# A hybrid transformer block: order of the first transfers, of one bank's release, and of three small steps at the head of its first attention

## The chip, the cores and the metric

The kernel runs on one core of one Trainium2 chip. The metric is the device time of one execution in microseconds; three executions of the kernel before took 2060.63 us in the median (2058.62 to 2062.41). All times below are in us from the first instruction of one profiled execution unless they are marked as ns.

Five engines work from queues of their own: TensorE (PE, matrix products), VectorE (DVE), ScalarE (ACT), GpSimd (POOL, here mostly an issuer of transfers) and SyncE (SP, here the issuer of all weight transfers). They meet only through semaphores.

## The reference, cut to what matters

One sequence of 256 tokens with 1024 features goes through two layers of a first model (latent attention and dilated attention, each with a modulated norm and an MLP), and then through a second block with a recurrent mixer, cross attention and a large expert layer. The change touches only the beginning of the first layer:

```python
cond = silu(c)
mod = (cond @ ada_w[0] + ada_b[0]).reshape(B, 6, D)      # shift1, scale1, gate1, ...
h = rms_norm(x, norm_mix[0]) * (1 + scale1) + shift1
proj = h @ w_in                                          # 1024 -> 384 + 256 + 32
q_lat, kv_lat, k_rope = split(proj);  k_rope = rope(k_rope, pos)
q  = (rms_norm(q_lat, g_qa) @ w_qb)                      # 16 heads of 96
kv = (rms_norm(kv_lat, g_kva) @ w_kvb)                   # 16 heads of 64 + 64
```

Attention over 16 heads, its output projection, and everything else follow.

## The kernel before, in words

All of it is one straight program for each engine, written out by hand; no scheduler moves anything. Activations are kept transposed: `xT` holds the input as 8 pieces of 128 features by 256 tokens. Every weight matrix is cut into units of up to 128x1024. SP loads unit u into one of four raw buffers (`weights(u)`, which from the fifth unit on waits until the split of unit u-3 is done), ACT copies it into a rounded high part `wh` (L1338), and DVE takes the rest into a low part `wl` (L1957). PE forms each product as high times high, high times low and low times high. The split runs two units ahead of the products.

**The start.** ACT issues five small transfers (L1431 to L1435): the condition as a column `c_col` (4 KB), the constants `con` (265 KB, among them a 128x128 block of ones and the identity), the positions `posI` (1 KB), the vectors `vec` (106.5 KB, biases and gains) and the condition as rows `cond` (512 KB). SP issues the input `xT`, and then the modulation weights and the first weight units (`early` and `weights`, L2876 and L2881).

**The first norm.** ACT squares features 0 to 511 of `xT` and DVE features 512 to 1023, both into `na` (marks `("n0","sq",0)` and `("n0","sq",1)`). PE sums the squares over the features with eight products by the block of ones; a float32 product stands in the trace as two matmuls, so these are 16. ACT and DVE make the root from it, and DVE scales `xT` into `na`.

**The modulation.** For feature pieces 0, 1, 3 and 5 the shift and the scale are made on PE (`ada(j)`, 8 products with `c_col`, 16 matmuls in the trace, then `columns(j)`). For pieces 2, 4, 6 and 7 DVE makes them by two multiply-and-sum instructions of 128x1024 on the weights in `first` (`products(j)`, L1940). PE runs sum of squares, `ada(0)`, `ada(1)`, `columns(0)`, `columns(1)`, `ada(3)`, `w_in(0)`, `columns(3)`, `w_in(1)`, `ada(5)`, `w_in(2)`, and so on to `w_in(7)`. Each `w_in(k)` needs the normed piece k in a high and a low part (`high(k)` on ACT, `low(k)` on DVE).

**The latent stage.** The eight `w_in` steps add up five latent tiles in five PSUM banks (`lat` 3 and 4 for keys and values, 0 to 2 for queries; bank 2 holds the raw rotary key as well). ACT and DVE take each tile out as a high and a low part (`latTh`, `latTl`), ACT squares the tiles, PE sums the squares (`lat_sums`), and the roots follow (`lat_root`). PE then runs the four units of `w_kvb`, two groups of products each (`kvb`, s, t), with the sums of squares and the turning of the rotary key (`k_rope`, L818) in between. ACT takes each group out with the root as its scale (mark `("kvb","v",s,t)`).

**The banks.** PSUM has eight banks. `take` in the tensor program takes the bank that stands first in a line of free banks and waits for whoever must have read it; `give` puts a bank at the end of the line, with the mark to be waited for. Which bank, and thus which wait, a step gets depends on the order of all `give` calls before it. Around the change the line is used so: `("kvb",0,0)` takes bank 3, the sums for keys and values bank 4, `("kvb",0,1)` bank 5, `k_rope` bank 6 (which held `lat` 3), `("kvb",1,0)` bank 7 (which held `lat` 4), and the sums for the queries bank 3.

**POOL** starts its own transfers only when the last of the sixteen `early` transfers has landed.

Of the kernel before, what the change touches and what calls it, by code (L numbers as in the profile page):

```python
# [8 lines left out]
ALU = mybir.AluOpType  # L9
# [537 lines left out]
def tensor_program(e, b, S, at):  # L547
    pe = Engine(e)
# [4 lines left out]
    def take(*name):  # L553

        i, sem, key = free.popleft()
        if sem is not None:
            pe.wait_ge(sem, at[key])
        at[("bank",) + name] = i
        return b.psum[:, i, :]

    def give(*name, sem, key):
        free.append((at[("bank",) + name], sem, key))

    def mm(o, l, r, start, stop, mark=None, loose=False):
        i = e.matmul(o, l, r, start=start, stop=stop, skip_group_check=loose)  # L565
        if mark:
            i.then_inc(S.pe, 1)
            n[0] += 1
            at[mark] = n[0]
# [195 lines left out]
    def mla():  # L765
        m = b.mla
# [68 lines left out]
        def kv(s):  # L835
            j = weights("mla_w_kvb", s)
            for t in range(2):
                ps = take("kvb", s, t)
                for k in range(2):
                    pe.wait_ge(S.dve, at["lat", "lo", 3 + k])  # L840
                    l, r = sp(m.latT, 3 + k, 256, t * 128, 128), wsp(j, k * 512, 512)
                    mm(ps, l[0], r[0], k == 0, False)
                    mm(ps, l[0], r[1], False, False)
                    if t == 1 and k == 1:
                        e.matmul(ps, l[1], r[0], start=False, stop=True).then_inc(S.unit, 1)
                    else:
                        mm(ps, l[1], r[0], False, k == 1, mark=("kvb", s, t) if k == 1 else None)
                if (s, t) == (0, 0):
                    for c in (3, 4):
                        give("lat", c, sem=S.act, key=("lat", "square", c))  # L850
                give("kvb", s, t, sem=S.act, key=("kvb", "v", s, t))
                if (s, t) == (0, 0):
                    lat_sums("kv", (3, 4), 0)
                if (s, t) == (0, 1):
                    k_rope()
                if (s, t) == (1, 0):
                    lat_sums("q", (0, 1, 2), 1)
# [83 lines left out]
            give("mla", "oT", c, sem=S.dve, key=("mla", "out", c))  # L941

        pe.wait_ge(S.c_con, 16)
        ps = take("n0", "sum")
        for k in (0, 1, 2, 3, 4, 5, 6, 7):
            if k < 4:
# [372 lines left out]
def scalar_program(e, b, S, at, d):  # L1319
# [5 lines left out]
    def act(o, i, f, mark=None, **kw):  # L1325
        e.activation(o, i, f, **kw).then_inc(S.act, 1)  # L1326
        n[0] += 1
        if mark:
            at[mark] = n[0]
        return n[0]  # L1330
# [98 lines left out]
    def mla():  # L1429
        m = b.mla  # L1430
        e.dma_start(m.ccol, d["c_col"]).then_inc(S.c_col, 16)  # L1431
        e.dma_start(b.con, d["con"]).then_inc(S.c_con, 16)
        e.dma_start(m.posI, d["pos_col"]).then_inc(S.pos_col, 16)
        e.dma_start(b.vec, d["vec"]).then_inc(S.c_vec, 16)
        e.dma_start(b.cond, d["c_row"]).then_inc(S.c_cond, 16)  # L1435
        ac.wait_ge(S.c_col, 16)
        act(m.ccol, m.ccol, ACT.Silu, mark="c col")
        ac.wait_ge(S.c_x, 16)
        act(m.na[:, 0:1024], b.xT[:, 0:1024], ACT.Square, mark=("n0", "sq", 0))
        ac.wait_ge(S.c_cond, 16)  # L1440
        act(b.cond, b.cond, ACT.Silu, mark=("cond",))
        ac.wait_ge(S.dve, at["angles"])
        act(m.trig, m.trig, ACT.Sin, mark=("trig",))
        ac.wait_ge(S.c_con, 16)
        norm_tail("n0", 8, m.ntmp)
        ac.wait_ge(S.c_vec, 16)

        def row(j):
            ac.wait_ge(S.pe, at["ada done", j])
# [39 lines left out]
        ac.wait_ge(S.unit, u + 1)  # L1489
        lat_high(2)  # L1490
        act(m.krT[0:32, :], bank("lat", 2)[0:32, 256:512], ACT.Copy, mark="k rope in")
        lat_root("kv", 2, 256)
        for c in range(3):
            lat_square(c)

        def head_root(key, z):
            h = m.hs[key]
# [414 lines left out]
def vector_program(e, b, S, at):  # L1912
# [15 lines left out]
    def tt(o, x, y, f, mark=None):  # L1928
        return op(e.tensor_tensor(o, x, y, f), mark)  # L1929
# [203 lines left out]

    def mla():
        m = b.mla
        ve.wait_ge(S.c_x, 16)
        tt(m.na[:, 1024:2048], b.xT[:, 1024:2048], b.xT[:, 1024:2048], ALU.mult, mark=("n0", "sq", 1))
        ve.wait_ge(S.c_con, 16)
        ve.wait_ge(S.pos_col, 16)
        cp(m.pos, m.posI)  # L2140
# [19 lines left out]
        ts(m.trig, m.trig, 3.1415925, -3.1415925, ALU.min, ALU.max, mark="angles")  # L2160
        ve.wait_ge(S.c_vec, 16)
        stt(m.more, vc(b, "ada_b", 8, 8), 1.0, vc(b, "norm_mix", 0, 8), ALU.add, ALU.mult)

        def product(c, slot):
            u = m.first[:, slot * UNIT:(slot + 1) * UNIT]
# [34 lines left out]
        for j in range(8):  # L2200
            if j >= 3:
                ada(j)
            ahead(j - AHEAD)
            low(j)
            if j in (1, 2, 3):
                products({1: 4, 2: 6, 3: 7}[j])
        unit("mla_w_in", 6)
        unit("mla_w_in", 7)

        def lat_low(c):  # L2210
            ve.wait_ge(S.act, at["k rope in"] if c == 2 else at["lat", "hi", c])
# [17 lines left out]
        for c in (3, 4, 0, 1, 2):  # L2229
            lat_low(c)  # L2230
        lat_root("kv", 2)
        ve.wait_ge(S.act, at["trig",])
        sin, cos = m.trig[:, 0], m.trig[:, 1]
        for h in range(2):
            cp(m.cs[:, :, 16 * h:16 * h + 16], cos)
        ts(m.sn[:, :, 0:16], sin, -1.0, None, ALU.mult)
        cp(m.sn[:, :, 16:32], sin)

        def kv(s):
            unit("mla_w_kvb", s)  # L2240
# [628 lines left out]
def sync_program(e, b, S, at, d, out):  # L2869
# [16 lines left out]
        early(2 * j + 1)  # L2886
    for j in range(3):
        weights(j)
    early(6)
    early(7)  # L2890
    weights(3)
    for i in range(8, 16):
        early(i)
    for j in range(4, 8):
        weights(j)
    for u in range(8, len(PLAN)):
        weights(u)
# [231 lines left out]
```

## Time and profile before

| | |
|---|---|
| median of three executions | 2060.63 us (2058.62 to 2062.41) |
| the profiled execution | 2060.63 us, of which its span is 2058.8 us |
| PE busy | 1983.9 us, 96% of the span |
| DVE busy | 1409.6 us, 68% |
| ACT busy | 1140.9 us, 55% |
| POOL busy | 302.1 us, 15% |
| mean granted PE clock | 0.984 of full |

The span runs from the first to the last instruction; 1.8 us of the execution lie around it. A PE that is shown busy is not PE at its peak, since matmuls are pipelined and their ends are modelled; what can be read well is when a matmul starts and whether PE waited before it. The stretch that the change touches is the first 60 us of the 2059.

### The profile page before, as it was taken

What the parts mean: (1) busy time and instruction counts of PE and PEld (TensorE: products, weight loads), DVE (VectorE), ACT (ScalarE), POOL (GpSimd) and SP (SyncE); (2) the same over time, 40 slices, a digit from 0 to 9 for tenths busy, and PEclk for the clock granted to TensorE, in tenths of its full rate; (3) what the DMA queues carried; (4) which work ended last, traced back from release to release, by engine and by line L of the source; (5) the groups of instructions that cost most, each with busy time, mean ns of one, the idle gap of its engine ahead of it and who ended that gap; (6) DMA issues with size and microseconds to landing.
All of it is one profiled execution on the core that took longest, in us unless ns stands there. A gap on an engine that the chain in (4) does not pass through costs nothing.

```text
span 2058.8 us, 34870 instructions
## 1 busy us (share of the span) xinstructions
PE 1983.9 (96%) x14212; PEld 1834.5 (89%) x14212; DVE 1409.6 (68%) x2543; ACT 1140.9 (55%) x1919; POOL 302.1 (15%) x328
## 2 busy tenths in 40 slices
PE   8998998999999989998898989999999999999997
PEld 5898998998888889997788989999999998888886
DVE  6777765888677567547646458999997765555554
ACT  5855533556766455435554444457767754444444
POOL 0010000000000000000000000018876950000000
PEclk9999999999999999999999999999999999999999
DMA  9465787346444347664334345554444445555553
GB/s 352 164 206 183 246 283 236 114 162 213 148 144 157 97 127 226 189 188 166 132 103 143 124 145 165 183 183 147 153 154 154 144 146 189 188 185 191 186 186 120
DMA packets 97743, 356.25 MB, mean 173 GB/s; under 512 B 11104, under 2 KB 11232, under 8 KB 97200
## 3 DMA queue, kind: packets, MB, share of 16 engines
q1 hardware_dynamic: 84240, 305.04, 44.5%
q0 software_dynamic: 12624, 48.08, 7.2%
q8 instruction: 112, 1.84, 0.3%
q10 hardware_dynamic: 720, 0.91, 0.1%
q14 instruction: 47, 0.39, 0.1%
HBM read 352.94 MB, written 1.05 MB: 172 GB/s over the span
## 4 chain that ended last, share of the span: by engine, by line
PE 91%; DVE 4%; ACT 3%; issue 1%; DMA 1%; ACTq 0%; DVEq 0%; POOL 0%
PE psum L572 24%; PE psum L574 24%; PE psum L573 23%; PE psum L565 18%; PE psum L579 2%; DVE wl L1957 1%; ACT work L1326 0%; ACT wh L1338 0%; DMA araw<-in_ada_w 0%; DVE C L1937 0%; DMA con<-in_con 0%; ACT L1326 0%; DVE araw L1940 0%; DVE mlp_sq L1937 0%; DVE cross_sq L1937 0%
## 5 line engine op out<-in xcount | busy, mean ns | idle before, releaser
L1957 DVE TENSOR_TENSOR wl<-raw,wh 128x1024 fp32r<-128x1024 f32 (+1 forms) x566 | 687.5, 1218 | 437.8 <-ACT wh L1338 437.1
L1338 ACT ACTIVATE wh<-raw 128x1024 fp32r<-128x1024 f32 (+1 forms) x566 | 593.6, 1050 | 444.3 <-PE psum L574 407.3
L572 PE MATMUL psum<-peer_hh,wh 128*128 128x256 f32 x1152 | 332.8, 289 | 4.2 <-DVE peer_hl L1929 4.0
L574 PE MATMUL psum<-peer_hh,wl 128*128 128x256 f32 x1152 | 326.2, 283 | 0.0
L573 PE MATMUL psum<-peer_hl,wh 128*128 128x256 f32 x1152 | 324.1, 281 | 0.0
L572 PEld LDWEIGHTS psum<-peer_hh,wh 128*128 128x128 f32 x1152 | 217.4, 189 | 5.4 <-issue 4.4
L573 PEld LDWEIGHTS psum<-peer_hl,wh 128*128 128x128 f32 x1152 | 219.9, 191 | 0.0
L574 PEld LDWEIGHTS psum<-peer_hh,wl 128*128 128x128 f32 x1152 | 216.6, 188 | 0.0
L572 PE MATMUL psum<-wh,csh 128*128 128x512 f32 x512 | 202.9, 396 | 0.0
L574 PE MATMUL psum<-wh,csl 128*128 128x512 f32 x512 | 202.7, 396 | 0.0
L573 PE MATMUL psum<-wl,csh 128*128 128x512 f32 x512 | 202.7, 396 | 0.0
L2848 POOL TENSOR_SCALAR C<-con,selT 128x128 f32<-128x128 f32 x128 | 135.2, 1069 | 194.9 <-DVE selT L1944 172.8
L572 PE MATMUL psum<-mlp_hh,wh 128*128 128x256 f32 x512 | 148.3, 290 | 8.3 <-DVE mlp_hl L1937 8.3
L573 PE MATMUL psum<-mlp_hl,wh 128*128 128x256 f32 x512 | 146.2, 286 | 0.0
L574 PE MATMUL psum<-mlp_hh,wl 128*128 128x256 f32 x512 | 146.2, 286 | 0.0
L573 PE MATMUL psum<-h1l,wh 128*128 128x256 f32 x512 | 144.1, 281 | 0.0
L572 PE MATMUL psum<-h1h,wh 128*128 128x256 f32 x512 | 144.1, 281 | 0.0
L574 PE MATMUL psum<-h1h,wl 128*128 128x256 f32 x512 | 144.1, 281 | 0.0
L2774 POOL DMA_DIRECT2D araw<-in_ada_w x76 | 40.1, 529 | 692.6 <-DVE mod L1940 662.1
L574 PEld LDWEIGHTS psum<-wh,csl 128*128 128x128 f32 x512 | 96.4, 188 | 23.4
L573 PEld LDWEIGHTS psum<-wl,csh 128*128 128x128 f32 x512 | 96.3, 188 | 23.4
L572 PEld LDWEIGHTS psum<-wh,csh 128*128 128x128 f32 x512 | 96.3, 188 | 23.3
(455 smaller groups left out, 4675.3 us busy)
## 6 DMA issues: line engine op xcount, KB each, us to landing
raw<-in_mlp_w SPq DMA_DIRECT2D x128, 512.0 KB, 4.1
raw<-in_eu SPq DMA_DIRECT2D x128, 512.0 KB, 3.5
raw<-in_ev SPq DMA_DIRECT2D x128, 512.0 KB, 3.4
araw<-in_ada_w POOLq DMA_DIRECT2D x76, 512.0 KB, 4.8
raw<-in_dil_qk SPq DMA_DIRECT2D x48, 512.0 KB, 3.6
raw<-in_dil_v SPq DMA_DIRECT2D x24, 512.0 KB, 3.6
raw<-in_w_in SPq DMA_DIRECT2D x16, 512.0 KB, 3.4
raw<-in_w_query SPq DMA_DIRECT2D x16, 512.0 KB, 3.5
```

Of the source, the lines that this page charges most:

```text
L565: i = e.matmul(o, l, r, start=start, stop=stop, skip_group_check=loose)
L572: e.matmul(o, l[0], r[0], start=start, stop=False, skip_group_check=loose)
L573: e.matmul(o, l[0], r[1], start=False, stop=False, skip_group_check=loose)
L574: i = e.matmul(o, l[1], r[0], start=False, stop=stop, skip_group_check=loose)
L579: t = e.transpose(o, i, ident)
L1338: e.activation(b.wh[v % NSPLIT][:, 0:cols], b.raw[v % NRAW][:, 0:cols], ACT.Copy).then_inc(S.hi, 1)
L1957: e.tensor_tensor(b.wl[v % NSPLIT][:, 0:cols], b.raw[v % NRAW][:, 0:cols], b.wh[v % NSPLIT][:, 0:cols].bitcast(F32), ALU.subtract).then_in ...
L2774: e.dma_start(b.araw[i % 2], d["ada_w"][first + c]).then_inc(S.ada[i % 2], 16)
L2848: e.tensor_scalar(o1[:, i, :], iota, m.selT[:, 0, t:t + 1], m.selT[:, 2, t:t + 1], ALU.is_equal, ALU.mult).then_inc(S.pool, 1)
```

## The change

It has five parts. In the first, ACT issues `posI` ahead of `con`, and `cond` ahead of `vec`. In the second, PE waits for `vec` as well as `con` before its sum of squares, ACT waits for `con` and `vec` before it squares its half of `xT`, and DVE squares its half only after the angles of the rotary embedding and one small instruction on `vec`. In the third, SP issues the later `early` transfers in pairs between weight units, where before all of them went ahead of the fifth unit; DVE's `products(6)` and `products(7)` are each one step later. In the fourth, four small DVE copies of sine and cosine move from behind the key root to ahead of the `latTl` steps, and ACT squares the three query tiles before it makes the key root, not behind it. In the fifth, the bank of `("kvb",0,0)` is given back ahead of the banks of `lat` 3 and 4.

```diff
@@ tensor program
+                give("kvb", s, t, sem=S.act, key=("kvb", "v", s, t))
                 if (s, t) == (0, 0):
                     for c in (3, 4):
                         give("lat", c, sem=S.act, key=("lat", "square", c))
-                give("kvb", s, t, sem=S.act, key=("kvb", "v", s, t))
-                if (s, t) == (0, 0):
                     lat_sums("kv", (3, 4), 0)
@@
         pe.wait_ge(S.c_con, 16)
+        pe.wait_ge(S.c_vec, 16)
         ps = take("n0", "sum")
@@ scalar program
         e.dma_start(m.ccol, d["c_col"]).then_inc(S.c_col, 16)
+        e.dma_start(m.posI, d["pos_col"]).then_inc(S.pos_col, 16)
         e.dma_start(b.con, d["con"]).then_inc(S.c_con, 16)
-        e.dma_start(m.posI, d["pos_col"]).then_inc(S.pos_col, 16)
+        e.dma_start(b.cond, d["c_row"]).then_inc(S.c_cond, 16)
         e.dma_start(b.vec, d["vec"]).then_inc(S.c_vec, 16)
-        e.dma_start(b.cond, d["c_row"]).then_inc(S.c_cond, 16)
         ac.wait_ge(S.c_col, 16)
         act(m.ccol, m.ccol, ACT.Silu, mark="c col")
+        ac.wait_ge(S.c_con, 16)
+        ac.wait_ge(S.c_vec, 16)
         ac.wait_ge(S.c_x, 16)
         act(m.na[:, 0:1024], b.xT[:, 0:1024], ACT.Square, mark=("n0", "sq", 0))
...
-        lat_root("kv", 2, 256)
         for c in range(3):
             lat_square(c)
+        lat_root("kv", 2, 256)
@@ vector program
-        ve.wait_ge(S.c_x, 16)
-        tt(m.na[:, 1024:2048], b.xT[:, 1024:2048], b.xT[:, 1024:2048], ALU.mult, mark=("n0", "sq", 1))
         ve.wait_ge(S.c_con, 16)
         ve.wait_ge(S.pos_col, 16)
...
         stt(m.more, vc(b, "ada_b", 8, 8), 1.0, vc(b, "norm_mix", 0, 8), ALU.add, ALU.mult)
+        ve.wait_ge(S.c_x, 16)
+        tt(m.na[:, 1024:2048], b.xT[:, 1024:2048], b.xT[:, 1024:2048], ALU.mult, mark=("n0", "sq", 1))
...
-            if j in (1, 2, 3):
-                products({1: 4, 2: 6, 3: 7}[j])
+            if j in (1, 3, 4):
+                products({1: 4, 3: 6, 4: 7}[j])
@@ sync program
-    early(6)
-    early(7)
-    weights(3)
-    for i in range(8, 16):
-        early(i)
-    for j in range(4, 8):
+    for j in range(3, 8):
+        early(2 * j)
+        early(2 * j + 1)
         weights(j)
```

At the very start of ACT's program its instructions change as follows (`na` is the buffer of the squares; the names in brackets are the semaphores waited for, `s_vec` and `s_con` those of the two transfers).

```order
@@ -1,18 +1,17 @@
-L2938 UNCONDITIONAL_BRANCH [waits barrier_Pool_Activation_PE_DVE_SP_release]
+L2935 UNCONDITIONAL_BRANCH [waits barrier_Pool_Activation_PE_DVE_SP_release]
 L1431 DMA c_col<-in_c_col 128x8
-L1432 DMA con<-in_con 128x530
-L1433 DMA posI<-in_pos_col 128x2
-L1434 DMA vec<-in_vec 128x213
-L1435 DMA cond<-in_c_row 128x1024
+L1432 DMA posI<-in_pos_col 128x2
+L1433 DMA con<-in_con 128x530
+L1434 DMA cond<-in_c_row 128x1024
+L1435 DMA vec<-in_vec 128x213
```

The vectors are now the last of the five transfers, and the constants the third. On PE the first matmul of the program, the sum of squares, reads so:

```order
-L565 MATMUL psum<-na,con 128x256 [waits s_act,s_con]
+L565 MATMUL psum<-na,con 128x256 [waits s_act,s_vec,s_con]
 L565 MATMUL psum<-na,con 128x256 x3
 L565 MATMUL psum<-na,con 128x256 [waits s_dve]
```

Nothing is moved there; one more semaphore is waited for. Further on, DVE's steps between the splits of the last `w_in` units (`wl`) and the first split of the `kvb` stage stand so (`cos_cos` and `minus_plus_sin` are the copies for the rotary embedding, `latTl` the low parts of the latent tiles, `lat_sums` the key root):

```order
@@ -62,10 +62,10 @@
 L1929 TENSOR_TENSOR mla_hl<-na,mla_hh 128x256
 L1957 TENSOR_TENSOR wl<-raw,wh 128x1024 x2
+L1944 COPY cos_cos<-trig 128x2x16 x2
+L1933 TENSOR_SCALAR minus_plus_sin<-trig 128x2x16
+L1944 COPY minus_plus_sin<-trig 128x2x16
 L1937 SCALAR_TENSOR_TENSOR latTl<-psum,vec,latTh 128x256 x5
 L1929 TENSOR_TENSOR lat_sums<-lat_sums 128x2
 L1937 SCALAR_TENSOR_TENSOR lat_sums<-lat_sums 128x2 x2
-L1944 COPY cos_cos<-trig 128x2x16 x2
-L1933 TENSOR_SCALAR minus_plus_sin<-trig 128x2x16
-L1944 COPY minus_plus_sin<-trig 128x2x16
```

Four instructions are moved ahead of the five `latTl` steps. On ACT, in the same place of the program:

```order
 L1326 ACTIVATE latTh<-psum,vec 128x256 x3
 L1326 ACTIVATE ntmp<-psum 32x256
+L1326 ACTIVATE lat_squares<-psum 128x256 x3
 L1326 ACTIVATE lat_sums<-psum,con 128x2
 L1326 ACTIVATE lat_sums<-lat_sums 128x2
-L1326 ACTIVATE lat_squares<-psum 128x256 x3
 L1338 ACTIVATE wh<-raw 128x1024
 L1326 ACTIVATE kv<-psum,lat_sums 128x512 x2
```

The three squares stand ahead of the two steps of the key root. PE's own order in this stage is the same before and after, but the line of free banks isn't: `k_rope` now gets bank 3, which waits for ACT's copy of `("kvb",0,0)` (the first `kv<-psum,lat_sums` above), where before it got bank 6, which waits for the square of `lat` 3. `("kvb",1,0)` gets bank 6, and the query sums bank 7.

## Rows read from the trace of the kernel before

**Rows 1.** Waits of PE in the first 100 us: total, times, longest (us).

```profile
PE psum L565 <- DMA con<-in_con: 8.0, 1, 8.0
PE psum L579 <- ACT na L1326: 1.5, 1, 1.5
PE psum L565 <- DVE latTl L1937: 0.8, 1, 0.8
PE psum L789 <- ACT ada_row L1326: 0.3, 1, 0.3
```

**Rows 2.** Timeline of PE: start, length, instruction, idle before and its releaser.

```profile
8.00 6.27 PE L565 MATMUL psum<-na,con 128*128 128x256 f32 x16 [8.00 <-DMA con<-in_con]
14.19 7.07 PE L565 MATMUL psum<-first,c_col 128*1 128x256 f32 x32
```

**Rows 3.** First PE row in two narrow windows, from 9.0 and from 9.5.

```profile
9.01 1.49 PE L565 MATMUL psum<-na,con 128*128 128x256 f32 x3
9.44 1.49 PE L565 MATMUL psum<-na,con 128*128 128x256 f32 x3
```

**Rows 4.** Busy time by stretch: PE, PEld, DVE, ACT, POOL, PE clock, DMA share, GB/s.

```profile
10.00:20.00 10.00, 10.00 (x40) 5.41 (x39) 6.96 (x21) 3.63 (x6) 0.00 (x0) 1.00 1.03 416
```

**Rows 5.** Timeline of ACT and its queue, and of DVE, in the first 15 us.

```profile
2.13 0.83 ACTq L1434 DMA_DIRECT2D vec<-in_vec  x1
5.97 1.04 ACT L1326 ACTIVATE na<-xT 128x1024 f32<-128x1024 f32 x1
13.83 1.06 ACT L1326 ACTIVATE cond<-cond 128x1024 f32<-128x1024 f32 x1 [6.83 <-DMA cond<-in_c_row]
...
9.74 0.17 DVE L1944 CAST pos<-posI 128x2 f32<-128x2 int32 x1 [2.84 <-DMA posI<-in_pos_col]
```

**Rows 6.** Transfers issued, first 14 us: queue, count, size, us from issue to landing.

```profile
vec<-in_vec ACTq DMA_DIRECT2D x1, 106.5 KB, 9.1
```

**Rows 7.** Timelines of DVE and PE, 20 to 31 us; a transfer that nothing delays.

```profile
22.57 0.85 DVE L1957 TENSOR_TENSOR wl<-raw,wh 128x672 fp32r<-128x672 f32 x1
30.36 3.61 PE L565 MATMUL psum<-first,c_col 128*1 128x256 f32 x16
...
raw<-in_ev SPq DMA_DIRECT2D x128, 512.0 KB, 3.4
```

**Rows 8.** Timelines of DVE and PE, 33 to 41 us.

```profile
33.82 1.22 DVE L1940 CUSTOM_DVE_ANT_0 first<-first,cond 128x1024 f32<-128x1024 f32 x1
36.49 0.42 DVE L1929 TENSOR_TENSOR mla_hl<-na,mla_hh 128x256 fp32r<-128x256 f32 x1 [0.35 <-ACT mla_hh L1326]
40.82 0.27 PE L565 MATMUL psum<-mla_hh,wh 128*128 128x256 f32 x1
```

**Rows 9.** Timeline of DVE, 47 to 52 us.

```profile
47.56 0.87 DVE L1937 SCALAR_TENSOR_TENSOR latTl<-psum,vec,latTh 128x256 fp32r<-128x256 f32 x2
...
49.25 1.44 DVE L1937 SCALAR_TENSOR_TENSOR latTl<-psum,vec,latTh 128x256 fp32r<-128x256 f32 x3 [0.82 <-ACT latTh L1326]
...
51.64 0.26 DVE L1944 COPY cos_cos<-trig 128x32 f32<-128x32 f32 x2
...
51.90 0.17 DVE L1944 COPY minus_plus_sin<-trig 128x32 f32<-128x32 f32 x1
```

**Rows 10.** Timeline of ACT, 50 to 54 us.

```profile
50.64 0.26 ACT L1326 ACTIVATE lat_sums<-psum,con 128x2 f32<-128x2 f32 x1 [0.47 <-PE psum L565]
...
51.05 0.91 ACT L1326 ACTIVATE lat_squares<-psum 128x256 f32<-128x256 f32 x3
51.84 1.07 ACT L1338 ACTIVATE wh<-raw 128x1024 fp32r<-128x1024 f32 x1
52.78 1.28 ACT L1326 ACTIVATE kv<-psum,lat_sums 128x512 f32<-128x512 f32 x2
```

**Rows 11.** Timeline of PE, around 52 us.

```profile
52.02 0.30 PE L818 MATMUL psum<-con,ntmp 32*128 32x32 f32 x2
```

**Rows 12.** Busy time by stretch, as in rows 4, further on.

```profile
350.00:400.00 50.00, 44.31 (x340) 42.95 (x341) 43.04 (x94) 28.41 (x62) 1.59 (x3) 0.93 0.32 105
```

More of the change, by code:

```diff
@@ L1443, in mla @@
         act(m.trig, m.trig, ACT.Sin, mark=("trig",))
-        ac.wait_ge(S.c_con, 16)
         norm_tail("n0", 8, m.ntmp)
-        ac.wait_ge(S.c_vec, 16)
         def row(j):
@@ L2204, in mla @@
             low(j)
-            if j in (1, 2, 3):
-                products({1: 4, 2: 6, 3: 7}[j])
+            if j in (1, 3, 4):
+                products({1: 4, 3: 6, 4: 7}[j])
         unit("mla_w_in", 6)
+        ve.wait_ge(S.act, at["trig",])
+        sin, cos = m.trig[:, 0], m.trig[:, 1]
         unit("mla_w_in", 7)
+        for h in range(2):
+            cp(m.cs[:, :, 16 * h:16 * h + 16], cos)
+        ts(m.sn[:, :, 0:16], sin, -1.0, None, ALU.mult)
+        cp(m.sn[:, :, 16:32], sin)
         def lat_low(c):
@@ L2231, in mla @@
         lat_root("kv", 2)
[L2232 to L2237, printed above, removed]
         def kv(s):
```

## The prediction

> **What bounds the kernel now.** I read four views in this order: PE's waits in the first 100 us, PE's timeline there, the timelines of ACT and DVE beside it, and the transfers. PE's waits [rows 1] are a short list: 8.0 us at the start until the constants have landed, and then only 0.8 us on DVE's `latTl`, 1.5 us on ACT's exponentials and 0.3 us on a row. From 8.00 to 47 us PE goes from one matmul to the next. So each microsecond by which PE's first matmul moves is a microsecond of the end, unless some later wait on a fixed time swallows it; and the waits of that list are all on work that itself starts from PE. Between 10 and 20 us PE is busy 10.00 of 10.00 us, and the transfers run at 416 GB/s with their engines full [rows 4]. The transfers are thus the scarce thing of the first microseconds, but PE doesn't wait for them after 8.00.
>
> **First part: PE starts later.** Before, PE needs the constants and the two halves of squares. ACT's half starts at 5.97 and takes 1.04 [rows 5], so it is done by 7.0, and the constants are last, at 8.00 [rows 2]. After the change three things stand ahead of the first matmul: ACT's queue loads the vectors last; ACT squares only when they are there; PE waits for the squares.
>
> When do the vectors land? Before, ACT's five transfers land in the order of issue: constants 8.0, positions 9.7 (the cast that waits for them starts at 9.74), vectors 2.13 + 9.1 = 11.2, and the condition rows 13.8 [rows 2, 5, 6]. Each is some 2 us behind the one ahead, 1 KB of positions nearly like 265 KB of constants, so what counts is that they stand in one line beside SP's full queue. The five are the same after, and SP issues the same up to that time; only the order within the line differs. The last of the line therefore still lands at about 13.8, and the last is now `vec`: it moves from 11.2 to 13.8. This rests on the rows. The Trainium skill's DMA: Bandwidth & Descriptors (section on the SWDGE path, Arbitration) says the same as a mechanism: an engine round-robins between the queues packet by packet, and takes each queue's descriptors in order. The same page (HWDGE ordering) warns that a later transfer's semaphore may complete ahead of an earlier one's; no row here shows that, and I carry it as the fourth rival.
>
> ACT then squares: 13.83 + 1.04 = 14.87. A semaphore takes some 0.06, so PE starts at 14.93. DVE's half (1.2 us, behind a 0.16 us step on `vec`) ends at 15.2, and PE asks for it only four products later. PE's start moves by 14.93 - 8.00 = **6.93 us**.
>
> Nothing takes this back. The sum (16 matmuls, 6.27 us), `ada(0)` and `ada(1)` (32, 7.07 us) follow back to back [rows 2] and ask for nothing sooner than before; ACT's condition step ends at 15.9 and DVE's `products(2)` at 18.3, ahead of the sum's end at 21.2. The sum itself is uncertain. Its matmuls start 0.43 us apart [rows 3], those of `ada` 7.07/32 = 0.22, though the granted clock is shown as 1.00 of 2.4 GHz in the stretch of rows 4: the first matmuls run at half pace whatever that column says. If all 16 ran at 0.43 the sum would take 6.9 (+0.6), if all ran at 0.22 it would take 3.5 (-2.8). I take 6.27 again, since PE comes out of idleness in both. The skill's TensorE: Matmul & The Clock Gate (Part 1) has it that the throttled state is the default, activity releases it, and the number of slow matmuls varies from run to run; the slow pitch agrees, the granted column doesn't, and the sum stays with the rows.
>
> **Second part: SP's order, and `products` one step later.** The fifth weight unit waits until DVE's first split is done, 22.57 + 0.85 = 23.4 [rows 7], and now six `early` transfers are queued behind that wait, and behind three more like it. With the shift the first gate opens at 30.4. Behind it go 0.34 + 0.52 + 0.52 = 1.39 MB up to the pair for `ada(5)`; at 416 GB/s they take 3.3 us. A transfer of 512 KB that nothing delays lands 3.4 us after its issue [rows 7], 1.3 of which are its bytes at that rate, so some 2 us are latency, and the pair is there at 36.0. `ada(5)` starts at 30.36 + 6.93 = 37.3 [rows 7]. Slack 1.3 us. The last pair, three times 1.39 MB behind the gate, is there at 30.4 + 2 + 10.0 = 42.4, against `products(7)` behind `low(4)` at 36.49 + 0.3 + 6.93 = 43.7 [rows 8]. Slack 1.3 us.
>
> On DVE, `products(7)` (two instructions of 1.15 us) now stands between `low(4)` and `ada(5)`. DVE is free for it at 36.6 (unshifted), ends at 38.9, and three short steps (`ada(5)` on DVE, the high part on ACT, the low part on DVE) take some 1.7 us, as an estimate from the lengths of 0.2 to 0.6 us of such steps; the low part is there at about 40.6. `w_in(5)` starts at 40.82 [rows 8]. It fits by 0.2 us; the two steps behind it have more. I take 0. If either slack is gone, the price is what the pair is late: up to 2 us. Below nothing it can't come, since PE has no wait there to lose.
>
> POOL's start hangs on the last pair and comes about 2 us later against PE; its first use lies behind the latent stage. 0.
>
> **Third part: the latent stage.** PE ends `w_in` and waits 0.8 us for DVE's first `latTl`, which starts at 47.56 [rows 1, 9]. DVE now does the four sine and cosine copies first. Their starts are (51.90 - 51.64)/3 = 0.09 apart [rows 9], together 0.35 us, and all of it lies on PE's wait: +0.35. They could have stood in DVE's idle time ahead of its last split, but they are placed behind it.
>
> Then the bank. PE reaches `k_rope` at 52.02 [rows 11], after this change at 52.37. It now takes bank 3 and must wait for ACT's copy of the first `kvb` group. That copy starts at 52.78 and the two take 1.28 [rows 10], so the first ends at 53.4. Is it later than before, as the squares now stand ahead of the root? Before: root 0.41 us from 50.64, squares, and the split at 51.84. After: the squares wait for the last `latTl` (49.25 + 1.44 + 0.35 = 51.05 [rows 9]) and end at 51.45, the root follows until 51.85, the split starts as before. DVE's part of the root takes 0.5 (from ACT's end at 51.1 to the copies at 51.64 [rows 9]) and is done at 52.4, ahead of the split's end. So the copy still starts at 52.78, and its end plus a semaphore is 53.45. `k_rope` moves from 52.02 to 53.45: **+1.43 us** for the stage, 0.35 of it the copies. As a bound, if ACT's root is 0.5 later than I think, +1.9; if the copy is early, +1.1. The steps behind it take banks whose owners are done by then (the query sums take bank 7, whose square is made at the start of the stage), and PE runs on to 84 us without a wait in the list of before, so it is not given back.
>
> **The sum.** 6.93 + 0 + 1.43 = 8.36 us. The profiled execution before took 2060.63 us (span 2058.8 and 1.8 around it), the same as the median, so the forecast is 2069.0 us, 0.4% slower.
>
> **The rivals.**
> 1. The bank costs nothing, because ACT's copy comes sooner or PE is later anyway. For it: ACT has idle gaps ahead of 50.64 [rows 10]. Against it: the copy stands behind a split that is bound to its place. Then 2060.6 + 6.9 + 0.35 = 2067.9.
> 2. SP's gates bind: `ada(5)` or `products(7)` waits for its pair, and PE with it. For it: slacks of 1.3 and 0.2 us, and transfers with full engines. Price 2 us, so 2071.0. It decides where the pair lands later than 37.3.
> 3. Not slower: the PE clock. In nine of the 50 us stretches the mean granted clock is 0.93 to 0.97, as from 350 to 400 [rows 12]. 0.07 of 50 us is 7 us at half the clock, 1.2 GHz, so up to 3.5 us of work lost in each, some 30 us in all. A program that starts 8.4 us later might meet them otherwise; it decides at three of nine. Against it: each fall follows gaps of PE that move with PE, and three executions before lie within 3.8 us. Then 2060 or less. The skill's clock gate section, by which the point of change varies between runs, is the rule behind it.
> 4. `vec` overtakes the condition rows, whose piece of the line is 13.8 - 11.2 = 2.6 us. Then PE starts at 12.3, and the time is 2066.4. Against it: the four rows of the line.
>
> **How the numbers follow.** Forecast 0.73; rival 1 0.09; rival 2 0.09; rival 3 0.03; rival 4 0.06. The forecast's own range is 2066.8 to 2071.0 (sum of squares at -1.5 to +0.6, the stage at +-0.4, the median of three at +-1.5). Taking in rivals 1, 2 and 4 mostly, the range is 2066.0 to 2072.0. What a measurement can tell from no change is 0.2%, 4.1 us. All but rival 3 lie above 2064.7; leaving a part of rival 4 and of the spread: slower 0.93, within 0.2% 0.05, faster 0.02.
>
> **What would show it.** In the profile after: PE's first matmul at 14.9 with ACT's square as releaser (before 12.5: rival 4); ACT idle before its square until a transfer at 13.8; `ada(5)` at 37.3 without a wait (with one: rival 2); the first `latTl` at 54.8, PE's wait before it 1.2; a wait of 1.1 us ahead of `k_rope` at L818 with ACT's `kv` as releaser (none: rival 1). From 60 us on the two traces should differ by a constant 8.4. A constant that shrinks at a stretch with a fallen clock would speak for rival 3. I am wrong if PE starts by 9, or if something behind 100 us waits on a fixed time.

## The result and the profile after

The changed kernel takes 2071.78 us in the median of five executions (2069.62 to 2076.44), the kernel before beside it 2061.64 us. The ratio is 1.0055, 95% interval 1.004 to 1.0072: slower, by 10 to 11 us where 8.4 were forecast. The profiled execution took 2069.42 us (span 2067.6), 8.8 more than the one of before and a little less than the lowest of the five.

PE's waits in the first 110 us of the changed kernel, columns as in [rows 1]:

```profile
PE psum L565 <- ACT na L1326: 15.2, 1, 15.2
PE psum L565 <- DVE latTl L1937: 3.0, 1, 3.0
PE psum L579 <- ACT na L1326: 1.5, 1, 1.5
PE psum L818 <- ACT kv L1326: 1.0, 1, 1.0
PE psum L565 <- DVE mla_hl L1929: 0.6, 1, 0.6
PE psum L789 <- ACT ada_row L1326: 0.3, 1, 0.3
```

Against [rows 1] the start is 15.2 and not 8.0, the wait for `latTl` 3.0 and not 0.8, and two waits are new: 1.0 at `k_rope` (L818) and 0.6 in the `w_in` stage. The start and `k_rope` were forecast. The 0.6 and most of the 3.0 were not.

The start, from the timeline of ACT (as in [rows 5]):

```profile
14.00 1.06 ACT L1326 ACTIVATE na<-xT 128x1024 f32<-128x1024 f32 x1 [8.04 <-DMA vec<-in_vec]
```

from the timeline of PE (as in [rows 2]):

```profile
15.20 5.50 PE L565 MATMUL psum<-na,con 128*128 128x256 f32 x16 [15.20 <-ACT na L1326]
20.62 7.07 PE L565 MATMUL psum<-first,c_col 128*1 128x256 f32 x32
```

and from the list of transfers issued in the first 14 us (as in [rows 6]):

```profile
vec<-in_vec ACTq DMA_DIRECT2D x1, 106.5 KB, 11.0
```

ACT issues the vectors at 2.88, so they land at 2.88 + 11.0 = 13.9, and PE starts at 15.20. The sum of squares takes 5.50 us, not 6.27, so `ada(0)` begins 20.62 - 14.19 = 6.43 later.

Then DVE's timeline, where the rows of before had no wait on a transfer (as in [rows 8]):

```profile
39.39 1.22 DVE L1940 CUSTOM_DVE_ANT_0 first<-first,cond 128x1024 f32<-128x1024 f32 x1 [2.50 <-DMA first<-in_ada_w]
...
46.18 0.84 DVE L1957 TENSOR_TENSOR wl<-raw,wh 128x672 fp32r<-128x672 f32 x1
```

and ACT's, at the split of the second `kvb` unit:

```profile
54.35 1.06 ACT L1338 ACTIVATE wh<-raw 128x1024 fp32r<-128x1024 f32 x1 [2.31 <-DMA raw<-in_mla_w_kvb]
```

DVE waits 2.5 us for `products(6)`' first transfer, so `products(7)` and the split of the sixth `w_in` unit behind it (46.18, before 37.19) are late, and PE waits 0.56 for the low part of that piece. SP issues the second `kvb` unit only when this split is done, at 47.05. ACT gets it at 54.35, 7.3 us after its issue, where 512 KB took 3.4 alone [rows 7]. What stood between is POOL. Its queue's timeline:

```profile
44.27 1.23 POOL L2805 DMA_DIRECT2D ada_piece<-in_ada_k  x2 [43.84 <-DMA first<-in_ada_w]
45.49 1.05 POOL L2774 DMA_DIRECT2D araw<-in_ada_w  x2
```

SP's, at the second `kvb` unit:

```profile
47.05 0.33 SPq L2876 DMA_DIRECT2D raw<-in_mla_w_kvb  x1
```

What each queue moved (packets, MB, share of the 16 engines; q1 is SP's, q0 POOL's), first from 46.9 to 48, then from 49 to 50, then from 51 to 52 us:

```profile
q0 software_dynamic: 87, 0.33, 90.9%
...
q0 software_dynamic: 111, 0.42, 105.8%
...
q1 hardware_dynamic: 53, 0.22, 52.7%
q0 software_dynamic: 60, 0.21, 52.6%
```

POOL's four transfers (2 MB) are issued when the last `early` transfer has landed, at 43.84, and that now comes just ahead of the second `kvb` unit. Up to three microseconds after SP's issue POOL's queue still has the engines for itself.

The kernel before had the same collision, which its rows of waits don't show. POOL's start, SP's issue of the second `kvb` unit, and that unit's time to landing:

```profile
33.81 1.22 POOL L2805 DMA_DIRECT2D ada_piece<-in_ada_k  x2 [33.38 <-DMA first<-in_ada_w]
...
38.07 0.33 SPq L2876 DMA_DIRECT2D raw<-in_mla_w_kvb  x1
...
raw<-in_mla_w_kvb SPq DMA_DIRECT2D x1, 512.0 KB, 6.4
```

There the second unit landed at 44.5 and ACT took it at 45.32; the first, issued at 36.17, took 6.9 us and landed at 43.1, and ACT took it at 43.21. Both came just in time. In the changed kernel the second unit is issued 47.05 - 38.07 = 8.98 us later, 2.55 more than the start's 6.43, and takes 0.9 us longer; that is more than there was to spare.

The last rows are PE's at the first product of the `kvb` stage and at `k_rope` (as in [rows 11]):

```profile
57.55 0.48 PE L565 MATMUL psum<-wh,latTh 128*128 128x512 f32 x1 [2.99 <-DVE latTl L1937]
...
62.44 0.31 PE L818 MATMUL psum<-con,ntmp 32*128 32x32 f32 x2 [0.96 <-ACT kv L1326]
```

**How the shift runs.** All kernels split the same 566 weight units on DVE (`wl`, one instruction each), so the start of split n less the start of the same split in the kernel before tells how late a kernel is at that place. The text calls this the shift. Each column is one profiled execution against the one of before, in us (e6 is told at its own place):

| split (its start before) | after | e1 | e2 | e3 | e4 | e5 | e7 | e8 | e9 | e10 | e11 | e12 |
|---|---|---|---|---|---|---|---|---|---|---|---|---|
| 3rd `w_in` (27.5) | 6.43 | 6.70 | -0.14 | 6.00 | -1.10 | 7.37 | 6.20 | -0.96 | -0.57 | -1.12 | -0.51 | -0.90 |
| 2nd `kvb` (46.4) | 9.02 | 6.70 | 1.70 | 5.99 | 1.10 | 7.98 | 9.38 | -0.27 | 0.43 | 0.70 | 0.30 | 1.02 |
| 1st `qb` (60.2) | 10.41 | 6.73 | 4.78 | 7.37 | 2.96 | 9.37 | 13.95 | -0.23 | -1.65 | -1.38 | 0.30 | -1.06 |
| last (2041) | 8.80 | 5.60 | 6.37 | 8.07 | 0.98 | 7.45 | 16.29 | 0.43 | -0.85 | -1.22 | -1.09 | -2.36 |

The change costs 10.4 us by 60 us, and the profiled execution gives 1.6 back over the other 2000 us, in steps between stretches where it moves with a constant distance. From 60 us to the end nearly every kernel drifts by one or two us either way, whatever was edited, so the row at 60 us is the one to read for the edits and the medians are the ones to read for the time.

### The profile page after: what moved, and what is told of

It reads as the page before. It is cut to its first block, busy times and chain, and to the rows that moved or that the text cites. A ratio compares the mean times of both kernels' runs of the same rounds, so it can differ in the third digit from the quotient of the medians.

```text
span 2067.6 us, 34869 instructions
## 1 busy us (share of the span) xinstructions
PE 1983.9 (96%) x14212; PEld 1833.6 (89%) x14212; DVE 1410.4 (68%) x2543; ACT 1141.0 (55%) x1919; POOL 302.9 (15%) x328
## 4 chain that ended last, share of the span: by engine, by line
PE 88%; DVE 6%; ACT 3%; DMA 2%; issue 1%; ACTq 0%; DVEq 0%; SPq 0%
PE psum L572 23%; PE psum L574 23%; PE psum L573 23%; PE psum L565 16%; PE psum L579 2%; DVE wl L1957 1%; ACT wh L1338 1%; DMA vec<-in_vec 1%; ACT work L1326 0%; DMA first<-in_ada_w 0%; DMA araw<-in_ada_w 0%; DMA raw<-in_mla_w_kvb 0%; ACT na L1326 0%; DVE mix_sq L1937 0%; ACT L1326 0%
```

## The experiments

Medians are over all executions of a kernel, with the ratio to the kernel before on the same chip and its 95% interval. The experiments ran on several chips, where the kernel before had medians of 2060.39 to 2061.64 us, so it is the ratios that compare best.

**e1, the start alone.** The first part of the change put into the kernel before, nothing else:

```diff
+        e.dma_start(m.posI, ...)            # ahead of con; cond ahead of vec
         e.dma_start(b.con, d["con"]).then_inc(S.c_con, 16)
...
+        pe.wait_ge(S.c_vec, 16)             # PE, and ACT ahead of its square
```

> The kernel before with the first part alone (order of the five small transfers, the waits of PE and ACT on the vectors, DVE's square behind the angles). Theory T (start 6.4 us, second part 2.6 us, bank and copies 1.4 us, each by itself): PE starts at about 15.2, the sum of squares is somewhat shorter, and from the first split on everything is 6.4 us later, with 0.85 us of wait before the first kvb product and none in the w_in stage; the time is 2068.0. Rival R (the weight units come late because the whole start is late against the transfers): the kvb weights are waited for here too, and the shift grows to 9 us or more by the kvb stage, 2071.

Measured: 2066.26 us, 1.0026 (1.0016 to 1.0037). PE starts at 15.37, the shift is 6.7 us at all three early splits, the wait for `latTl` is 0.8 as before, and no weight unit is waited for. The start costs what it costs by itself; the late start makes no weight unit late, so rival R is refuted. The time is 1.7 us under theory T's 2068.0; by the end of the profiled execution the shift is 5.6.

**e2, SP's order and the products alone.**

```diff
-            if j in (1, 2, 3):
-                products({1: 4, 2: 6, 3: 7}[j])
+            if j in (1, 3, 4):
+                products({1: 4, 3: 6, 4: 7}[j])
...
-    early(6)
-    early(7)
-    weights(3)
-    for i in range(8, 16):
-        early(i)
-    for j in range(4, 8):
+    for j in range(3, 8):
+        early(2 * j)
+        early(2 * j + 1)
         weights(j)
```

> The kernel before with the second part alone (later early transfers in pairs between the gated weight units, products(6) and products(7) one step later). Theory T: PE starts at 8.0 as before, DVE waits some 2 us for the pair of products(6), w_in(5) waits about 0.7 us, POOL starts some 3 us later and its 2 MB collide with the second kvb unit, so the first kvb product is 2 to 3 us later than in the kernel before; the time is 2063.5 (2062.5 to 2065). Rival P (the prediction's zero: the slacks cover it, and the late transfers come only with the late start): no wait in w_in, the time is 2061.

Measured: 2065.46 us (2062.54 to 2071.10), 1.0023 (1.0014 to 1.0033). The zero of the prediction is refuted, but the median lies above theory T's range, and the shift at the first `qb` split, 4.78, is about double what the theory had. PE's waits:

```profile
PE psum L565 <- DVE latTl L1937: 2.3, 1, 2.3
```

and the busy time by stretch, columns as in [rows 4] (the granted clock, as a share of 2.4 GHz, is the third number from the end):

```profile
50.00:52.00 2.00, 2.00 (x6) 1.56 (x7) 1.10 (x4) 1.86 (x6) 0.00 (x0) 0.64 0.66 201
52.00:54.00 2.00, 2.00 (x10) 1.95 (x9) 0.39 (x1) 0.21 (x1) 0.00 (x0) 0.50 0.05 14
54.00:56.00 2.00, 2.00 (x6) 1.41 (x5) 0.83 (x7) 1.97 (x7) 0.00 (x0) 0.50 0.00 0
57.00:58.00 1.00, 1.00 (x4) 0.82 (x5) 0.88 (x8) 0.97 (x4) 0.00 (x0) 0.82 0.00 0
```

The wait of 2.3 us costs 1.5 more than before, and PE waits 0.2 in the `w_in` stage. Behind the long wait the granted clock falls to 0.50, 1.2 GHz, until 57 us, and the products of the `kvb` stage run at half pace; that is the other 3 us. Not every long wait brings this: the changed kernel's profile has a wait of 3.0 us and a granted clock of 1.00 behind it.

**e3, the changed kernel with the old order of SP and of the products** (the diff of e2 taken back).

> The changed kernel with its second part undone (SP's order and the place of the products as before). Theory T: 10.4 - 2.6 = 7.8 us later than the kernel before at the end of the latent stage, time 2069.2; PE's wait before the first kvb product is 1.2 us and not 3.0, and POOL starts at the same distance from PE's start as in the kernel before, or earlier. Rival R (the late weights come from the late start): 2071 to 2072 as in the changed kernel.

Measured: 2068.46 us, 1.0035 (1.0022 to 1.0047). The wait for `latTl` is 1.19, `k_rope` waits 0.95. At the first `qb` split the shift is 7.37: 6.00 from the start (the sum of squares took 5.1) and 1.37 from the latent stage. With SP's old order POOL starts at 32.64, and SP issues the second `kvb` unit at 44.07, 11.4 us behind it; it takes 4.0 us. The start is late here too and the unit is not, so rival R is refuted.

**e4, the bank and the copies alone.** The kernel before with

```diff
+                give("kvb", s, t, ...)       # ahead of give("lat", 3) and ("lat", 4)
...
+        cp(m.cs ...), ts(m.sn ...), cp(m.sn ...)   # behind unit("mla_w_in", 7)
```

> The kernel before with the bank's release and the sine and cosine copies moved as in the change, without ACT's squares ahead of the root. Theory T: the copies add 0.35 us to PE's wait before the first kvb product (0.85 to 1.2), k_rope waits 1.1 us for ACT's copy of the first kvb group; +1.4 us at the end of the stage, time 2062.6. Rival: the wait at the bank is hidden (k_rope without a wait), +0.35 us, 2061.3.

Measured: 2061.38 us, 1.0001 (0.9991 to 1.001). `k_rope` waits for the bank (1.42 us, 1.1 foreseen), so its rival is refuted in the trace, but the time doesn't resolve 1.4 us. The execution shows something else as well, in ACT's timeline at the first `kvb` unit:

```profile
45.19 1.06 ACT L1338 ACTIVATE wh<-raw 128x1024 fp32r<-128x1024 f32 x1 [1.97 <-DMA raw<-in_mla_w_kvb]
```

and in PE's:

```profile
38.33 0.36 PE L565 MATMUL psum<-mla_hh,wh 128*128 128x256 f32 x1 [0.61 <-DVE col L1937]
49.64 0.47 PE L565 MATMUL psum<-wh,latTh 128*128 128x512 f32 x1 [2.61 <-DVE latTl L1937]
54.99 0.30 PE L818 MATMUL psum<-con,ntmp 32*128 32x32 f32 x2 [1.42 <-ACT kv L1326]
```

The sum of squares took only 5.24 us, PE ran 1.1 us ahead, and ACT and DVE, and PE behind them, then waited for transfers that the edit doesn't touch (the first `kvb` unit took 7.7 us behind POOL's 2 MB). So the shift goes from -1.10 to 2.96, far more than the edit's 1.4. The profile of before, where no transfer was late, showed an execution at the edge. The granted clock stays at 1.00 behind the wait of 2.61.

**e5, the changed kernel with POOL held back.**

```diff
-        po.wait_ge(S.early[15], 16)
+        po.wait_ge(S.lo, 10)        # the second kvb unit is split
```

> The changed kernel, with POOL's first four transfers (2 MB) held back until the second kvb unit is split, in place of until the last early transfer has landed. Theory T (the second kvb unit is late because it shares the engines with POOL's 2 MB): PE's wait before the first kvb product falls from 3.0 to about 1.2 us, the shift at the end of the latent stage from 10.4 to about 8.6 us, and the spread between executions becomes smaller; time 2069.8. Rival G (the gates alone make it late: the second kvb unit is issued only when a split held up by products(7) is done): the wait stays near 3 us, time 2071.8.

Measured: 2067.95 us (2066.42 to 2069.63), 1.0036 (1.0023 to 1.0049). One line takes some 4 us off the changed kernel's median; the spread, over five and six executions, is 3 us and not 7. The two intervals (1.004 to 1.0072 and 1.0023 to 1.0049) overlap a little. PE's waits:

```profile
PE psum L565 <- DVE latTl L1937: 1.2, 1, 1.2
PE psum L818 <- ACT kv L1326: 1.0, 1, 1.0
PE psum L565 <- DVE mla_hl L1929: 0.4, 1, 0.4
```

The wait for `latTl` is 1.2: the kernel before's 0.85 and the copies' 0.35. SP still issues the second `kvb` unit 2.4 us late against the start, at 47.81 (47.81 - 38.07 - 7.37), but it takes 3.4 us and is there in time. What the queues moved from 48.5 to 49 us:

```profile
q1 hardware_dynamic: 14, 0.06, 71.6%
```

So without POOL's transfers the unit's first packets move at most 1.2 us after its issue; in the changed kernel there were none until 50.5, 3.4 us after it. The gates alone do not make the unit late. At the first `qb` split the shift is 9.37, of which 7.37 is the start (the sum of squares took 6.58), 1.4 the third part and 0.6 what is left of the second.

**e6, the kernel before with POOL held back** (the same line).

> The kernel before, with POOL's first four transfers held back until the second kvb unit is split. Theory T: in the profiled execution of before no weight unit was late, so the mean moves little; executions in which a kvb unit came late (as in the run with bank and copies moved, 2.6 us of wait) go away, so 2060.3 and a narrower spread. Rival: the transfers, now beside the units of the query stage, make those late: slower than 2062.

Measured: 2060.10 us, 0.9996 (0.9986 to 1.0006). The shift stays under 0.1 us to 60 us. The second `kvb` unit takes 4.5 us and not 6.4, and the query units don't suffer. No gain can be told. (One of its ten executions took 10607.85 us, which no trace explains; the ratio leaves it out, the median doesn't.)

**e7, the changed kernel, ACT squaring as soon as `con` is there.**

```diff
         ac.wait_ge(S.c_con, 16)
-        ac.wait_ge(S.c_vec, 16)
```

> The changed kernel, ACT squaring without waiting for the vectors; PE still waits for them, and DVE still squares behind its step on them. Theory T: PE's start is the landing of the vectors plus ACT's 1.05 us of squaring; without the wait it is the landing alone, 14.0 to 14.2 and not 15.2, so 1.1 us less for the start; DVE's half ends at 15.3, ahead of PE's fifth product. Time 2070.7. Rival (what PE gains at the start it gives back in the w_in stage, since there the gated transfers set the pace): the start moves, the time stays at 2071.8 within 0.5.

Measured: 2071.68 us, 1.0051 (1.0034 to 1.0068). PE starts at 14.13, released by the vectors themselves, 1.07 earlier, as both theories had it. The time stays, as the rival had it: four executions between 2069.19 and 2076.91 can't tell 1 us. The profiled one took 2076.91 and shows why. PE's waits:

```profile
PE psum L565 <- DVE latTl L1936: 3.1, 1, 3.1
...
PE psum L565 <- DVE mla_hl L1928: 1.0, 1, 1.0
```

and the stretch from 60 us, columns as in [rows 4]:

```profile
60.00:65.00 5.00, 5.00 (x16) 3.77 (x16) 2.08 (x5) 2.79 (x7) 0.00 (x0) 0.50 0.00 1
```

Of the 1.07 gained at the start the sum of squares, with 6.34 us in place of 5.50, happens to take 0.84; the 0.23 left is more than lost in the longer wait in `w_in` (1.0 and not 0.6). Behind the wait of 3.1 us the clock falls as in e2, here from 57 to 67 us: the shift is 13.95 at the first `qb` split. One profile can't separate the rival's account from this luck.

**e8, a warm start.** The kernel before, with PE busy on zeros until the constants land:

```diff
+        pe.wait_ge(S.dve, at["warm"])       # DVE has cleared 384 columns
+        for k in range(8):
+            mm(b.psum[:, 7, 0:256], m.row3[:, 0:128], m.row3[:, 128:384], True, True)
         pe.wait_ge(S.c_con, 16)
```

> The kernel before, with eight float32 products of zeros (16 matmuls of 256 columns) on PE while it waits for the constants, so that the sum of squares does not begin at half pace. Theory S (PE bounds the head): the sum of squares takes 3.5 us and not 6.3, everything is 2.5 us sooner, 2058.2. Rival D (the transfers of the head are at their limit too, as the run with bank and copies moved suggests, where PE was 1.1 us ahead and then waited for products(7) and for the first kvb unit): the lead of 2.7 us melts until the kvb stage to under 1 us, time 2060.

Measured: 2061.09 us, 0.9999 (0.999 to 1.0009). The sum takes 3.72 us in place of 6.27, and in the time nothing is left of the gain. PE's waits:

```profile
PE psum L565 <- DVE col L1940: 1.3, 1, 1.3
PE psum L565 <- DVE latTl L1940: 1.1, 1, 1.1
...
PE psum L565 <- DMA first<-in_ada_k: 0.4, 1, 0.4
```

In DVE's timeline a transfer is late:

```profile
30.87 1.23 DVE L1943 CUSTOM_DVE_ANT_0 first<-first,cond 128x1024 f32<-128x1024 f32 x1 [1.16 <-DMA first<-in_ada_w]
```

`ada(0)` starts 2.7 us sooner. The lead is 1.0 at the third `w_in` split and 0.2 at 60 us. PE waits 0.4 for a transfer itself, and DVE, from which it waits 1.3 for `col`, had waited 1.16 for one. Theory D holds: in the head of the kernel before the transfers are as near to being the limit as PE is.

**e9, the latent tiles first.** The kernel before, ACT's and DVE's split of the second `kvb` unit moved behind the first two latent tiles:

```diff
-        unit("mla_w_in", 7)
...
         for c in (3, 4, 0, 1, 2):
             lat_low(c)
+            if c == 4:
+                unit("mla_w_in", 7)
```

> The kernel before, with ACT's and DVE's split of the second kvb unit moved behind the first two latent tiles (key and value), which are done before PE ends w_in. Theory: the 0.85 us of PE's wait before the first kvb product goes, unless the first kvb unit's landing holds it; k_rope and the copies behind are not held. Shift at the end of the stage -0.8 us, time 2060.1. Rival: ACT and DVE, nearly full in this stage, come late with the second kvb unit, and the wait only moves: 2060.9.

Measured: 2060.96 us, 1.0000 (0.9991 to 1.0009). In the profile PE has no wait for `latTl` ahead of the `kvb` stage any more:

```profile
PE psum L565 <- DMA con<-in_con: 8.0, 1, 8.0
...
PE psum L789 <- ACT ada_row L1326: 0.3, 1, 0.3
```

The shift at 60 us is -1.65, 0.57 of it from a shorter sum, so the edit is worth 1.1. Not to be told in the time alone.

**e11, SP's order and the products alone, POOL held back** (e2 with e5's line).

> The kernel before with the change's second part (SP's order and the products' place), and POOL's first transfers held back. Theory T (of the second part's cost only the wait of w_in(5), 0.2 to 0.9 us, belongs to the gates; the rest is POOL's collision with the second kvb unit and the half clock that follows a long wait): 2061.5, no fall of the clock before 100 us. Rival G (the gates cost it all): 2065 as in the run with the second part alone.

Measured: 2059.99 us, 1.0002 (0.9992 to 1.0011), against e2's 2065.46. PE's waits:

```profile
PE psum L565 <- DVE latTl L1937: 0.8, 1, 0.8
PE psum L565 <- DVE mla_hl L1929: 0.6, 1, 0.6
```

This is the clearest of all: the same order of SP, DVE waiting 2.4 us for `products(6)`' transfer, and a wait in `w_in` even longer than e2's 0.2, yet the time is the kernel before's again, and the intervals of the two ratios don't overlap. From the third `w_in` split to 60 us the shift grows by 0.8 (-0.51 to 0.30), in e2 by 4.9. So nearly all that the second part costs goes away when POOL's transfers are out of the way.

**e10 and e12, all edits that help.** e12 is the kernel before with e6's and e9's edits; e10 has the warm start besides.

> The kernel before with the warm start of PE, POOL's first transfers held back, and the latent split moved. Theory D (the transfers limit the head up to products(7), then PE does): with the POOL transfers out of the way the first kvb units are early, so of the 2.7 us of the warm start about 0.3 to 1.5 us survive, plus 0.8 from the latent split: 2059.0. Theory S (PE alone bounds the head): 2057.3.

> The kernel before with POOL's first transfers held back and the latent split moved, without the warm start. Theory: -0.8 us from the split and a few tenths in the mean from the kvb units that no longer come late: 2059.6, faster than before and than either alone. Rival: nothing beyond the spread, 2060.8.

Measured: e12 2058.93 us, 0.9991 (0.9982 to 1.0); e10 2058.60 us, 0.9991 (0.9982 to 1.0). Both medians lie 1.5 to 1.8 us under the kernel before's and the intervals just touch no change, so whether they are faster than it is at the limit of what can be told; they are clearly faster than the changed kernel. The warm start adds nothing that can be told.

## Why the prediction was right and wrong

**What bounds the head: half right.** The statement that "PE doesn't wait for them after 8.00" was true of the one execution shown, and was taken for slack. e4 and e8 show that a PE which is 1.1 to 2.7 us ahead waits for transfers, so the kernel before has PE and the transfers nearly level. Its own trace has the sign of it: the first two `kvb` units took 6.9 and 6.4 us, not 3.4, and landed 0.1 and 0.9 us before ACT took them. That one-sided view did no harm to the first term, since a later PE only gets further behind the transfers (e1: no new wait).

**First part: right.** Forecast +6.93 for PE's start, measured +7.20: the vectors landed at 13.9 (forecast 13.8), and ACT's square is the releaser in e1, e3 and the changed kernel alike; PE starts 0.14 us after that square's end at 15.06, where 0.06 was taken. The line of five transfers kept its total length, so the fourth rival, the overtaking, did not happen. The sum of squares was taken as unchanged and took 5.50; over the profiles it took 5.1 to 6.6 without any edit to it. Net 6.43 (6.0 to 7.4). The shorter sum, 7.20 less 6.43, is luck.

**Second part: the step that failed.** The prediction "took 0", from two slacks of 1.3 us against the landing of the pairs, and of POOL's start it said "its first use lies behind the latent stage. 0." Measured in the profile after: the first `kvb` product starts 57.55 - 48.19 = 9.36 us later. Of that 6.43 is the start and 0.35 the copies. The rest is the second part's: 0.79 us in `w_in` (0.56 of it the wait) and 1.79 us more wait ahead of the `kvb` stage, 2.6 together. Between the medians of the changed kernel and e3 lie 3.3 us (2071.78 and 2068.46), less well known, as the intervals overlap. Its size is about what the forecast of 2069.0 lacks against 2071.78.

There were two errors. The landing was worked out for the pair of `ada(5)` and the last pair, and not for the pair between them, that of `products(6)`. The prediction's own sum gives 30.4 + 2 + 6.7 = 39.1 for it; `products(6)` starts at 39.39, and DVE had been free since 36.89. So DVE is 2.5 us late, the split of the sixth `w_in` unit with it, and with that split SP's issue of the second `kvb` unit. And of POOL's transfers it was asked only who needs them, and not whom they get in the way of. Its start hangs on the last `early` transfer, and with the pairs delayed its 2 MB come 2.8 us ahead of that unit's issue, where with SP's old order and the same late start (e3) it was 11.4.

It takes both. In the kernel before, POOL stood 4.3 us ahead of a unit that was issued in time, and the unit came just in time. In e5 and e11, with the gates in place and POOL held back, the unit is issued 2.4 and 2.6 us late against the start and is in time all the same, and the cost goes down to 0.6 and 0.8 us in the profiles. POOL's later start by itself, with every split in time, was not run. The second rival named a price near this (2071.0), but not the mechanism: PE had `ada(5)` at 36.78 without a wait, and the pairs' landing alone cost no more than those 0.6 to 0.8.

**Third part: right.** Forecast +1.43, measured 0.35 by the copies and 1.06 at `k_rope`, 1.41 together. From the third `w_in` split to 60 us the shift of e3 grows by 1.37 and that of e1 by 0.03. ACT's squares ahead of the root cost nothing that shows: with them (e3) `k_rope` waits 0.95, as in the changed kernel.

**The third rival, the clock, exists with the other sign.** The prediction spoke of the clock only as something that might give time back. In e2 and e7 it fell to 0.50 behind a wait of 2.3 and 3.1 us and cost some 3 us. It did not fall behind a wait of 3.0 in the changed kernel's profiled execution, nor behind one of 2.6 in e4. What decides it is not shown. That the slowest of the changed kernel's executions (2076.44) had such a fall is a guess from e7's 2076.91, which had one; no trace of that execution was seen.

**The constant distance behind 60 us: wrong in detail.** The distance of the profiled execution shrank from 10.4 to 8.8. Edits that touch only the head drift alike (e11 from 0.3 to -1.1), so this seems to be what two executions differ by anyway; what it comes from was not looked into.

## What to carry to other kernels

When a step is moved that another engine's start hangs on, ask not only who needs that engine's work but what its transfers will then collide with; the price of a transfer is paid by the one behind it. A profile without a wait on a transfer does not show slack: look at how long the transfers took and when they landed, for an engine and the transfers can be level. Work out the landing of every moved transfer, not of the first and the last. And a new wait of some microseconds on TensorE may be paid twice, by itself and by the clock behind it.

## What the runs showed of the hardware

A transfer from SP that was issued behind 2 MB of POOL's was not served alongside. Between 49 and 50 us, 2 us after SP's issue, POOL's queue had 111 packets and SP's none, where with POOL held back (e5) SP's first packets moved at most 1.2 us after the issue. From 50 to 51 they had 100 and 11, from 51 to 52 an even share, and SP's 512 KB took 7.3 us against 3.4 alone. The Trainium skill's DMA: Bandwidth & Descriptors (Queues, rings and completion order, Arbitration) has the engines take turns between queues packet by packet, a packet being typically 9 to 17 descriptors. The even share from 51 to 52 us agrees with turns. The rows before it neither agree nor disagree clearly: the profile's packets are of some 3.8 KB (0.42 MB in 111), and from 48.2, 1.2 us after the issue, to 50.5 POOL's queue moved 252 of them, some 16 on each of the 16 engines. If each is one descriptor, that is a single turn by the page's figure; that they are is not shown.

The first matmuls of the program run at half pace for a time that differs by execution: the same 16 took between 5.14 (e3) and 6.58 us (e5), 6.27 in the profile of before, while 16 behind a warm-up took 3.72. The granted clock is shown as 1.00 in all of this, and the prediction took that for a contradiction. It is none. The list of clock changes in the trace of before begins at 13.18 us, with the full clock, and a stretch ahead of the first entry is shown as 1.00. Of the 16 matmuls the 12 that start before 13.18 are 0.43 us apart (0.59 after the first) and the others 0.22. All the traces have it so: in the changed kernel's the list begins at 18.86, in e3's at 18.06 and in e5's at 20.90, and there the spacing changes, after 9, 7 and 14 matmuls.
